# Layer norm by sums per token: shifted values, scalars as 128x4, and a spread by products with diagonals

## The chip, the cores and the metric

One core of a Trainium2 chip runs the whole program once. The metric is the time of an execution on the device in microseconds (us). Five engines work side by side, each through its own queue in order, and hand over to each other by semaphores: TensorE (PE, matrix products into PSUM banks), VectorE (DVE), ScalarE (ACT), GpSimd (POOL) and SyncE (SP), which only issues DMAs here.

## The reference

512 tokens of width 1024 pass through two layers (a pooling mixer and a sliding-window attention, each with a convolved, gated feed-forward of width 2816), a final norm, and a third layer: a conformer convolution and a squared-relu MLP of width 4096. The change is in the conformer convolution:

```
def layer_norm(x, g, b):
    mu = jnp.mean(x32, axis=-1, keepdims=True)
    xc = x32 - mu
    y = xc * lax.rsqrt(jnp.mean(xc * xc, axis=-1, keepdims=True) + RMS_EPS)
    return (y * g + b)
def conformer_conv(x, w_in, b_in, conv_w, conv_b, ln_g, ln_b, w_out, b_out):
    a, g = jnp.split(x @ w_in + b_in, 2, axis=-1)
    h = a * jax.nn.sigmoid(g)
    h = depthwise causal convolution of h over 31 tokens, + conv_b
    h = jax.nn.silu(layer_norm(h, ln_g, ln_b))
    return h @ w_out + b_out
```

## The kernel before

Activations lie with the 1024 features on partitions, as 8 chunks of 128 features x 512 tokens. Each f32 operand of a large product is split in a high part (`whi`, `xh`, rounded to fp32r by ACT, L799) and a low part (`wlo`, `xl`, the difference, by DVE, L1137), and a product is three (L475 to L477). A unit of weights is 128x1024; a chain is the 24 products of a unit, into one of the banks `acc[0..3]`. Weight units go through four slots: SP loads, ACT makes `whi`, DVE makes `wlo`.

The stage "ain" loops over the chunks c = 0 to 7 on every engine. PE (L755): the two chains of chunk c (values and gate), then `convolve(c - 1)`, then one product of ones with `hv` of chunk c - 2 into `norm[0]` (L751), which adds up the mean over all features, the same in every partition. DVE (L1509): evicts the two chains (L1527, `tmp`), makes the gated value `hc` (L1533), its low part `hcl` (L1545), and its share of the 31 taps. ACT (L1079): splits, the gate's sigmoid (L1091), `hch`, the high part of `hc` (L1100), the products of POOL's taps (`tapped`, L1074), and, for the convolution on PE, for each tap two 128x128 diagonals (L1059, L1061). POOL adds up `tapped` (L462). The 31 taps are divided by hand: `PE_TAPS`, `POOL_TAPS`, `LATE_TAPS` (done by DVE on the convolution's bank) and the rest, `own_taps`, on DVE in `bank[5]` (L1485 the first, L1488 the others). `collect` (L1500) adds the three partial sums to `hv` of the chunk.

After the loop the layer norm: the mean is subtracted from the eight chunks (L1555, DVE), ACT squares them (L1113), POOL and DVE add up some of the squares (L467, L1561), and PE sums them by products with ones (L770); root (L1115), reciprocal of 128x512 (L1564), a product for each chunk (L1567), Silu with slope and offset per feature (L1118), high and low parts `yhi` (L1121) and `ylo` (L1570, L1574). PE then runs the output projection "aout": its first two chains go feature block by feature block as `ylo` arrives (L775), the other six one after another. The reciprocal of `r1` (L1576), wanted by the residual in `finish` (L1168), stands behind the layer norm on DVE. Then follows the MLP.

A product of an f32 operand that isn't fp32r is shown as two instructions (two passes). At the very start of the kernel `token_sums` (L562) makes sums per token: the 128 features x 128 tokens of a block are the weights, and four columns (`pick`, one of them ones) are streamed.

Of the kernel before, what the change touches and what calls it, by code (L numbers as in the profile page):

```python
# [42 lines left out]
PE_TAPS = (9, 8, 7, 7, 7, 7, 12, 13)  # L43
POOL_TAPS = (11, 11, 11, 11, 11, 11, 10, 5)
# [105 lines left out]
def build(nc, xT, vec_in, cst_in, w_in, out):  # L150
# [3 lines left out]
    with ExitStack() as ctx:  # L154
# [37 lines left out]
        with ExitStack() as own:  # L192
# [4 lines left out]
            dgh = sb("dgh", [P, 2, max(PE_TAPS) * P], F32R, own)  # L197
            dgl = sb("dgl", [P, 2, max(PE_TAPS) * P], F32R, own)
# [10 lines left out]
        gfm = sb("gfm", [P, C])  # L209
        pbs = sb("pbs", [P, C])  # L210
# [5 lines left out]
        sq = sb("sq", [P, 2, T])  # L216
        u = sb("u", [P, 4, 2 + T])
# [7 lines left out]
        taps = bank[5]  # L225
# [66 lines left out]
        xc_ready = sem("xc_ready")  # L292
        xcsq_ready = sem("xcsq_ready")
        early_pair = sem("early_pair")
        late_sums = sem("late_sums")
# [40 lines left out]

        NORMS = ["pool", "ffn0", "qkv", "ffn1", "ain", "mlp"]
# [7 lines left out]
        RR = {"pool": 0, "ffn0": 1, "qkv": 2, "ffn1": 3, "ain": 4, "mlp": 7}  # L345
# [69 lines left out]
        def _(pool):  # L415
# [50 lines left out]
            pool.wait_ge(xcsq_ready, 4)  # L466
            nc.gpsimd.tensor_tensor(square_of(2), square_of(2), square_of(3), ALU.add).then_inc(early_pair, 1)  # L467
# [4 lines left out]
        def _(pe):  # L472
# [262 lines left out]
            def convolve(c):  # L735
# [5 lines left out]
                for k in range(PE_TAPS[c]):  # L741
                    w = slice(k * P, (k + 1) * P)
                    mm = three(bank[6 + b][:], dgh[:, b, w], dgl[:, b, w], hch[:, b, k:k + T],
                               hcl[:, b, k:k + T], k == 0, k == PE_TAPS[c] - 1)
                mm.then_inc(conv_done, 1)

            def feature_sum(c):
                if c == 0:
                    pe.wait_ge(rms_ready, RR["ain"] + 2)
                pe.wait_ge(hv_ready, c + 1)  # L750
                mm = nc.tensor.matmul(norm[0][:], ones[:], hv[:, c, :], start=(c == 0), stop=(c == C - 1))  # L751
                if c == C - 1:
                    mm.then_inc(mean_done, 1)
# [12 lines left out]
            feature_sum(C - 1)  # L766
# [361 lines left out]
        def _(dve):  # L1128
# [380 lines left out]
            for c in range(C):  # L1509
# [39 lines left out]
                if c:  # L1549
                    collect(c - 1)  # L1550
# [109 lines left out]
```

## Time and profile before

| | |
|---|---|
| time, median of 3 runs | 1498.51 us (1497.73 to 1498.73) |
| the profiled execution | 1498.34 us, of which span 1496.2 |
| busy PE / DVE / ACT / POOL | 98% / 63% / 44% / 14% |
| granted TensorE clock, mean | 0.994 |
| stage "ain" to the end of its last convolution | about 940 to 1078.5 us |
| from there to the first product of "aout" | to 1098.68 us |

A timeline row is: start us, length us, engine, line, operation, output<-inputs, shape, count, and in brackets how long the engine had sat idle before it and what released it. "x4" are four instructions merged. The granted clock is a share of 2.4 GHz.

### The profile page before, as it was taken

To read this page: it belongs to the slowest core of one execution; us is meant where nothing else is said; L and a number is where in the kernel's file an instruction comes from. 1 tells how busy PE (TensorE), PEld (TensorE's weight loads), DVE (VectorE), ACT (ScalarE), POOL (GpSimd) and SP (SyncE) were. 2 spreads that over 40 slices of the span, in tenths; PEclk is the share of its full clock that TensorE was granted. 3 is DMA by queue.
4 is the path that set the end of the run, shared out by engine and by line. 5 is a ranking of instruction groups with operands and counts; after the bars stand their busy time and mean duration, and the time that the engine had idled before them with its cause. 6 is when DMAs were issued, how large, how long until landed. Compare 5 with 4: busy or idle time off the path is not lost.

```text
span 1496.2 us, 20225 instructions
## 1 busy us (share of the span) xinstructions
PE 1463.8 (98%) x6878; PEld 1204.8 (81%) x6878; DVE 941.7 (63%) x1350; ACT 655.3 (44%) x1064; POOL 215.7 (14%) x155
## 2 busy tenths in 40 slices
PE   7999999999999999999999999999779999999999
PEld 7888888888877898888888887777558888888887
DVE  6877774573555667767735735898888763544532
ACT  5444441341546664444413415888754322222210
POOL 1200000000302241000000006498612000000000
PEclk9999999999999999999999999999989999999999
DMA  5222223232322012332332323111112322232321
GB/s 185 71 98 99 98 98 113 76 107 74 123 92 65 29 58 85 99 101 95 99 113 80 104 72 109 57 57 57 39 45 100 113 98 99 91 106 84 105 99 49
DMA packets 38956, 132.45 MB, mean 89 GB/s; under 512 B 4208, under 2 KB 4464, under 8 KB 38896
## 3 DMA queue, kind: packets, MB, share of 16 engines
q1 hardware_dynamic: 37888, 128.99, 26.2%
q10 hardware_dynamic: 1008, 2.69, 0.5%
q8 instruction: 35, 0.57, 0.2%
q14 instruction: 25, 0.20, 0.0%
HBM read 129.56 MB, written 2.10 MB: 88 GB/s over the span
## 4 chain that ended last, share of the span: by engine, by line
PE 85%; POOL 7%; ACT 4%; DVE 2%; issue 1%; ACTq 0%; POOLq 0%; DVEq 0%
PE bank L475 27%; PE bank L476 26%; PE bank L477 26%; POOL prod L462 5%; POOL ssum L434 2%; PE bank L557 1%; PE bank L618 1%; PE bank L646 1%; PE bank L631 1%; ACT dgl L1061 1%; ACT dgh L1059 1%; PE bank L580 1%; DVE bank L1488 1%; ACT whi L799 0%; ACT tapped L1074 0%
## 5 line engine op out<-in xcount | busy, mean ns | idle before, releaser
L475 PE MATMUL bank<-xh,whi 128*128 128x512 f32 x1184 | 465.9, 394 | 1.4 <-DVE res L1423 0.7
L477 PE MATMUL bank<-xh,wlo 128*128 128x512 f32 x1184 | 460.8, 389 | 0.0
L476 PE MATMUL bank<-xl,whi 128*128 128x512 f32 x1184 | 460.7, 389 | 0.0
L799 ACT ACTIVATE whi<-raw 128x1024 fp32r<-128x1024 f32 x244 | 255.7, 1050 | 232.6 <-PE bank L477 232.5
L1137 DVE TENSOR_TENSOR wlo<-raw,whi 128x1024 fp32r<-128x1024 f32 x244 | 305.4, 1252 | 57.0 <-ACT whi L799 49.4
L475 PEld LDWEIGHTS bank<-xh,whi 128*128 128x128 f32 x1184 | 222.3, 188 | 50.8 <-issue 3.1
L476 PEld LDWEIGHTS bank<-xl,whi 128*128 128x128 f32 x1184 | 222.3, 188 | 48.0 <-issue 2.4
L477 PEld LDWEIGHTS bank<-xh,wlo 128*128 128x128 f32 x1184 | 222.3, 188 | 46.4
L475 PE MATMUL bank<-ahi,whi 128*128 128x512 f32 x608 | 236.5, 389 | 0.0
L476 PE MATMUL bank<-alo,whi 128*128 128x512 f32 x608 | 236.5, 389 | 0.0
L477 PE MATMUL bank<-ahi,wlo 128*128 128x512 f32 x608 | 236.5, 389 | 0.0
L1158 DVE TENSOR_TENSOR res<-bank,res 128x512 f32 (+1 forms) x80 | 55.3, 691 | 201.5 <-PE bank L477 201.5
L434 POOL TENSOR_TENSOR ssum<-ssum,sq 128x512 f32<-128x512 f32 x40 | 62.4, 1561 | 759.4 <-ACT sq L818 418.8
L1208 DVE SCALAR_TENSOR_TENSOR tmp<-u,vec,tmp 128x512 f32<-128x512 f32 x176 | 124.2, 748 | 29.0 <-ACT tmp L856 28.9
L477 PEld LDWEIGHTS bank<-ahi,wlo 128*128 128x128 f32 x608 | 114.1, 188 | 23.8
L475 PEld LDWEIGHTS bank<-ahi,whi 128*128 128x128 f32 x608 | 114.1, 188 | 23.7
L476 PEld LDWEIGHTS bank<-alo,whi 128*128 128x128 f32 x608 | 114.1, 188 | 23.6
L856 ACT ACTIVATE tmp<-u,vec 128x512 f32<-128x512 f32 x88 | 71.7, 815 | 126.8 <-DVE u L1203 126.7
L1203 DVE TENSOR_TENSOR u<-bank,rinv 128x512 f32<-128x512 f32 x88 | 59.7, 686 | 68.4 <-PE bank L477 68.4
L462 POOL TENSOR_TENSOR prod<-prod,tapped 128x512 f32<-128x512 f32 x65 | 99.2, 1526 | 18.6 <-ACT tapped L1074 9.7
L878 ACT ACTIVATE ahi<-tmp 128x512 f32 (+1 forms) x32 | 20.2, 632 | 121.9 <-DVE tmp L1233 121.9
L860 ACT ACTIVATE gate<-tmp 128x512 f32<-128x512 f32 x44 | 27.9, 634 | 96.3 <-DVE tmp L1208 96.3
(175 smaller groups left out, 1439.2 us busy)
## 6 DMA issues: line engine op xcount, KB each, us to landing
raw<-w_ffn_up SPq DMA_DIRECT2D x88, 512.0 KB, 3.3
raw<-w_ffn_down SPq DMA_DIRECT2D x32, 512.0 KB, 3.3
raw<-w_mlp_up SPq DMA_DIRECT2D x32, 512.0 KB, 3.3
raw<-w_mlp_down SPq DMA_DIRECT2D x32, 512.0 KB, 3.3
raw<-w_ain SPq DMA_DIRECT2D x16, 512.0 KB, 3.3
raw<-w_ffn_down SPq DMA_DIRECT2D x16, 384.0 KB, 3.0
raw<-w_qkv SPq DMA_DIRECT2D x12, 512.0 KB, 3.2
raw<-w_wo SPq DMA_DIRECT2D x8, 512.0 KB, 3.3
```

Source lines behind the costliest of these rows:

```text
L434: nc.gpsimd.tensor_tensor(ssum[:, which, :], ssum[:, which, :], sq[:, buf, :], ALU.add)\
L462: nc.gpsimd.tensor_tensor(prod[:, c % 2, :], a, tapped[:, (made + k) % PARTS, :], ALU.add)\
L475: nc.tensor.matmul(out_, hi, mh, start=first, stop=False)
L476: nc.tensor.matmul(out_, hi, ml, start=False, stop=False)
L477: return nc.tensor.matmul(out_, lo, mh, start=False, stop=last)
L799: nc.scalar.activation(whi[:, s, 0:tiles * P], raw[:, s, 0:tiles * P], ACT.Copy)\
L856: nc.scalar.activation(tmp[:, k, :], u[:, k, 2:2 + T], ACT.Identity, scale=col(vec, par + 2), bias=col(vec, par + 3))\
L860: nc.scalar.activation(gate[:, b, :], tmp[:, 2 * b + 1, :], ACT.Silu)\
L1137: V.tensor_tensor(wlo[:, s, 0:tiles * P], raw[:, s, 0:tiles * P], whi[:, s, 0:tiles * P].bitcast(F32), ALU.subtract).then_inc(lo_done, 1)
L1158: V.tensor_tensor(row(res, c), acc[k][:], row(res, c), ALU.add).then_inc(acc_free, 1)
L1203: V.tensor_tensor(u[:, k, 2:2 + T], acc[k][:], rinv[:], ALU.mult).then_inc(acc_free, 1)
L1208: V.scalar_tensor_tensor(tmp[:, k, :], u[:, k, shift:shift + T], col(vec, par + 4 * j + shift), tmp[:, k, :], op0=ALU.mult, op1=ALU.add).t ...
```

## The change

- Chunk 0's mean (one product of ones with `hv` of chunk 0, in `norm[1]`, PE's loop step c = 2) is a common shift. DVE puts minus this mean in `rms`; the first own tap of chunks 2 to 7 becomes `hc * w + rms`, so that their `hv` come out shifted. Chunks 0 and 1 are shifted afterwards by DVE, in step c = 7.
- Sums of values and of squares are taken per token, like `token_sums`: sixteen groups of four products with eight streamed columns of `one_of`, into `norm[0][:, 0:8]`. Groups 0 to 3 stand in PE's steps c = 4 to 7 in the place of the mean products, groups 4 to 7 ahead of `convolve(7)`, groups 8 to 15 behind it. ACT makes the squares of chunks 2, 3, 0 and 1 in its step c = 7, the others after the loop; they lie in `sq` and `ssum`.
- Mean, variance, root, slope and offset are 128x4. Slope and offset are spread over partitions: DVE and ACT make diagonals of them, and PE multiplies ones with these into banks 5 and 6. A chunk is then a product and a sum on DVE (L1567 alone before).
- The own taps add up in `acc[0]` or `acc[2]`, with a wait of PE on `tap_steps` ahead of the chains; chunk 7 has 15 taps on PE (13 before), 4 on POOL (5), 12 own (13); two of its diagonals lie in storage of their own.
- "aout" runs three chains block by block, not two, after units 1 to 3 are split (1 and 2 before).
- The reciprocal of `r1` moves to DVE's step c = 0, after its own taps. The pair sums of squares on POOL and DVE, and the reciprocal of 128x512, go.

The core of the diff:

```diff
-PE_TAPS = (9, 8, 7, 7, 7, 7, 12, 13)
-POOL_TAPS = (11, 11, 11, 11, 11, 11, 10, 5)
+PE_TAPS = (9, 8, 7, 7, 7, 7, 12, 15)
+SPARE_TAPS = 2
+SHIFTED = 2
+POOL_TAPS = (11, 11, 11, 11, 11, 11, 10, 4)
...
+        SQUARES = (2, 3, 0, 1, 4, 5, 6, 7)
+        FIRST, SECOND = range(NBLK), range(NBLK, 2 * NBLK)
+        STATISTICS = [(2, FIRST), (3, FIRST), (4, FIRST), (5, FIRST), (2, SECOND), (3, SECOND), (0, FIRST),
+                      (0, SECOND), (1, FIRST), (1, SECOND), (4, SECOND), (5, SECOND), (6, FIRST), (6, SECOND),
+                      (7, FIRST), (7, SECOND)]
...
+                for b in range(NBLK):
+                    mm = nc.tensor.matmul(norm[0][:, 0:2 * NBLK], x[:, b * P:(b + 1) * P], pick_token_block(which[b]),
+                                          start=(n == 0 and b == 0), stop=(n == 2 * C - 1 and b == NBLK - 1))
+                mm.then_inc(sums_done, 1)
...
+                if c >= 2:
+                    pe.wait_ge(tap_steps, own_steps(c - 1))
                 for k in (2 * (c % 2), 2 * (c % 2) + 1) if c else ():
                     chain(p, c // 2, k, xh, xl)
                 if c >= 1:
                     convolve(c - 1)
-                if c >= 2:
-                    feature_sum(c - 2)
+                if c == 2:
+                    shift_sum()
+                if c >= 4:
+                    token_statistics(c - 4)
+            for n in range(4, 8):
+                token_statistics(n)
             convolve(C - 1)
-            feature_sum(C - 2)
-            feature_sum(C - 1)
...
+            for n in range(8, 2 * C):
+                token_statistics(n)
+
+            for at, ready, e in ((bank[5], slope_ready, 0), (bank[6], offset_ready, 1)):
+                for b in range(NBLK):
+                    pe.wait_ge(ready, b + 1)
+                    mm = nc.tensor.matmul(at[:, b * P:(b + 1) * P], ones[:], spread[:, e, b, :], start=True, stop=True)
+                mm.then_inc(spread_done, 1)
...
-                for k in range(2):
+                for k in range(3):
...
                 if c == C - 1:
                     products(c - 1, range(PARTS, POOL_TAPS[c - 1]))
+                    for e in SQUARES[0:3]:
+                        square(e)
                 products(c, range(min(PARTS, POOL_TAPS[c])))
...
+                if n == 0 and c < SHIFTED:
+                    V.tensor_scalar(part, x, w, None, ALU.mult).then_inc(tap_steps, 1)
                     return
...
+                V.scalar_tensor_tensor(hv[:, c, :] if n == len(own_taps(c)) - 1 else part, x, w,
+                                       part if n else rms[:], op0=ALU.mult, op1=ALU.add).then_inc(tap_steps, 1)
...
                 if c:
                     collect(c - 1)
+                if c == 0:
+                    V.reciprocal(r1[:], r1[:]).then_inc(rinv_ready, 1)
             collect(C - 1)
...
+            for b in range(NBLK):
+                V.tensor_scalar(spread[:, 0, b, :], ident, ln_slope[:, b:b + 1], None, ALU.mult).then_inc(slope_ready, 1)
+            split_lo(p.unit, 0, 2 * C - 1 + AHEAD)
             for c in range(C):
+                dve.wait_ge(spread_done, 1)
+                V.tensor_tensor(hv[:, c, :], hv[:, c, :], bank[5][:], ALU.mult).then_inc(ln_mul, 1)
+                dve.wait_ge(ln_mul, c + 1)
+                dve.wait_ge(spread_done, 2)
+                V.tensor_tensor(hv[:, c, :], hv[:, c, :], bank[6][:], ALU.add).then_inc(ln_scaled, 1)
```

## Rows read from the trace of the kernel before

**Rows 1.** page, part 1: busy us (share of the span) and instructions
```profile
PE 1463.8 (98%) x6878; PEld 1204.8 (81%) x6878; DVE 941.7 (63%) x1350; ACT 655.3 (44%) x1064; POOL 215.7 (14%) x155
```

**Rows 2.** windows: us; busy us (count) of PE, PEld, DVE, ACT, POOL; clock; DMA; GB/s
```profile
1010.00:1030.00 20.00, 19.92 (x86) 15.75 (x85) 19.35 (x25) 17.33 (x35) 18.57 (x12) 1.00 0.24 80
1067.50:1071.00 3.50, 3.41 (x8) 2.70 (x9) 3.43 (x6) 3.50 (x6) 3.21 (x3) 0.54 0.00 0
```

**Rows 3.** timeline of PE around the last convolution: start us, us, instruction, count, idle before
```profile
1063.74 1.02 PE L751 MATMUL bank<-hv,ones 128*128 128x512 f32 x2
...
1067.59 0.66 PE L475 MATMUL bank<-hch,dgh 128*128 128x512 f32 x1 [2.83 <-DVE hcl L1545]
...
1071.34 0.40 PE L475 MATMUL bank<-hch,dgh 128*128 128x512 f32 x1
...
1078.13 0.40 PE L477 MATMUL bank<-hch,dgl 128*128 128x512 f32 x1
...
1098.68 0.77 PE L475 MATMUL bank<-yhi,whi 128*128 128x512 f32 x1 [7.22 <-DVE ylo L1570]
```

**Rows 4.** timeline of POOL: the add before which it waited, first adds of two chunks
```profile
960.94 8.25 POOL L462 TENSOR_TENSOR prod<-prod,tapped 128x512 f32<-128x512 f32 x5 [2.41 <-ACT tapped L1074]
...
1020.02 1.30 POOL L462 TENSOR_TENSOR prod<-tapped 128x512 f32<-128x512 f32 x1
...
1037.03 1.30 POOL L462 TENSOR_TENSOR prod<-tapped 128x512 f32<-128x512 f32 x1
```

**Rows 5.** timelines of DVE and ACT: chunk 1's eviction and gate, and `r1`
```profile
956.00 1.28 DVE L1527 TENSOR_TENSOR tmp<-bank,rinv 128x512 f32<-128x512 f32 x2
...
958.59 0.71 ACT L1091 ACTIVATE gate<-tmp,vec 128x512 f32<-128x512 f32 x1
...
960.15 1.32 ACT L1074 ACTIVATE tapped<-hc,vec 128x512 f32<-128x512 f32 x2
...
1108.05 3.35 DVE L1576 RECIPROCAL r<-r 128x512 f32<-128x512 f32 x1
```

**Rows 6.** by line: duration ns min/median/max, first and last start, forms
```profile
L1533 DVE SCALAR_TENSOR_TENSOR hc<-tmp,vec,gate x8: 747/1268/1792, 947.8 to 1065.3; 128x512 f32<-128x512 f32 x8
...
L1485 DVE TENSOR_SCALAR bank<-hc,vec x8: 753/754/755, 948.6 to 1066.1; 128x512 f32<-128x512 f32 x8
```

**Rows 7.** timelines of DVE and POOL within one chunk
```profile
1025.91 1.35 DVE L1137 TENSOR_TENSOR wlo<-raw,whi 128x1024 fp32r<-128x1024 f32 x1 [0.40 <-ACT whi L799]
...
1027.18 1.78 DVE L1533 SCALAR_TENSOR_TENSOR hc<-tmp,vec,gate 128x512 f32<-128x512 f32 x1
...
1028.56 1.57 POOL L462 TENSOR_TENSOR prod<-prod,tapped 128x512 f32<-128x512 f32 x1
```

**Rows 8.** timeline of ACT: first diagonal, gate and products of chunk 7, four squares
```profile
1056.99 0.39 ACT L1059 ACTIVATE dgh<-cst,cwh 128x128 fp32r<-128x128 f32 x1
...
1064.60 0.71 ACT L1091 ACTIVATE gate<-tmp,vec 128x512 f32<-128x512 f32 x1
...
1066.68 5.70 ACT L1074 ACTIVATE tapped<-hc,vec 128x512 f32<-128x512 f32 x9
...
1085.15 2.42 ACT L1113 ACTIVATE tmp<-hv 128x512 f32<-128x512 f32 x4
```

**Rows 9.** timelines of PE, ACT and DVE at the start: sums by token, small steps
```profile
17.45 0.95 PE L566 MATMUL bank<-pick,sq 128*128 128x4 f32 x8
...
19.15 3.70 PE L557 MATMUL bank<-wg,res 128*128 128x256 f32 x16
...
24.57 0.26 ACT L943 ACTIVATE rms<-bank,eps 128x4 f32<-128x4 f32 x1 [5.58 <-PE bank L566]
...
24.86 0.18 DVE L1342 RECIPROCAL rinv<-rms 128x4 f32<-128x4 f32 x1 [4.10 <-ACT rms L943]
```

**Rows 10.** timeline of DVE in the layer norm: a split and a product
```profile
1090.20 1.22 DVE L1137 TENSOR_TENSOR wlo<-raw,whi 128x1024 fp32r<-128x1024 f32 x1
...
1098.46 0.68 DVE L1567 TENSOR_TENSOR hv<-hv,rinv 128x512 f32<-128x512 f32 x1
```

More of the change, by code:

```diff
@@ L209, in build @@
         gfm = sb("gfm", [P, C])
+        with ExitStack() as own:
+            one_of = sb("one_of", [P, 4 * NBLK], F32, own)
         pbs = sb("pbs", [P, C])
@@ L216, in build @@
         sq = sb("sq", [P, 2, T])
+        with ExitStack() as own:
+            dgh7 = sb("dgh7", [P, SPARE_TAPS * P], F32R, own)
+            dgl7 = sb("dgl7", [P, SPARE_TAPS * P], F32R, own)
         u = sb("u", [P, 4, 2 + T])
@@ L782, in _ @@
                         mm.then_inc(chain_done, 1)
-            for k in range(2, p.units):
+            for k in range(3, p.units):
                 chain(p, k // SLOTS, k % SLOTS, yhi, ylo)
@@ L1088, in _ @@
                     act.wait_ge(taps_split, 2)
-                    diagonals(0)
+                    diagonals(0, range(PE_TAPS[0]))
                 act.wait_ge(acc_free, p.chain + 2 * c + 2)
@@ L1110, in _ @@
             nc.scalar.activation(eps[:, 4:5], eps[:, 0:1], ACT.Sqrt)
-            for c in range(C):
-                act.wait_ge(xc_ready, c + 1)
-                nc.scalar.activation(square_of(c), hv[:, c, :], ACT.Square).then_inc(xcsq_ready, 1)
-            act.wait_ge(sqsum_done, 2)
-            nc.scalar.activation(rms[:], norm[1][:], ACT.Sqrt, scale=1.0 / D, bias=eps[:, 0:1]).then_inc(rms_ready, 1)
+            for e in SQUARES[4:]:
+                square(e)
+            act.wait_ge(ln_steps, 3)
+            nc.scalar.activation(ln_rms, ln_var, ACT.Sqrt, bias=eps[:, 0:1]).then_inc(ln_root, 1)
+            act.wait_ge(ln_steps, 5)
+            for b in range(NBLK):
+                nc.scalar.activation(spread[:, 1, b, :], ident, ACT.Copy, scale=ln_offset[:, b:b + 1])\
+                    .then_inc(offset_ready, 1)
+            nc.scalar.activation(eps[:, 4:5], eps[:, 0:1], ACT.Silu)
             for c in range(C):
@@ L1502, in collect @@
                 dve.wait_ge(tapped_steps, sum(POOL_TAPS[:c + 1]) - c - 1)
-                dve.wait_ge(tap_steps, sum(len(own_taps(j)) for j in range(c + 1)))
+                dve.wait_ge(tap_steps, own_steps(c + 1))
                 V.tensor_tensor(hv[:, c, :], prod[:, c % 2, :], hv[:, c, :], ALU.add).then_inc(late_steps, 1)
@@ L1529, in _ @@
                     split_lo(p.unit, 0, 2 * c + AHEAD)
+                if c == SHIFTED:
+                    dve.wait_ge(mean_done, 1)
+                    V.tensor_scalar(rms[:], norm[1][:], -1.0 / P, None, ALU.mult).then_inc(shift_ready, 1)
+                    dve.wait_ge(shift_ready, 3)
+                if c == C - 1:
+                    for e in range(SHIFTED):
+                        V.scalar_tensor_tensor(hv[:, e, :], norm[1][:], -1.0 / P, hv[:, e, :],
+                                               op0=ALU.mult, op1=ALU.add).then_inc(xc_ready, 1)
                 dve.wait_ge(sig_ready, c + 1)
@@ L1562, in _ @@
-            split_lo(p.unit, 0, 2 * C - 1 + AHEAD)
-            dve.wait_ge(rms_ready, RR["mlp"])
-            V.reciprocal(rinv[:], rms[:]).then_inc(rinv_ready, 1)
-            dve.wait_ge(rinv_ready, 8)
-            for c in range(C):
-                V.tensor_tensor(hv[:, c, :], hv[:, c, :], rinv[:], ALU.mult).then_inc(ln_scaled, 1)
+            dve.wait_ge(sums_done, 2 * C)
+            V.tensor_scalar(ln_mean, norm[0][:, 0:NBLK], 1.0 / D, None, ALU.mult).then_inc(ln_steps, 1)
+            dve.wait_ge(ln_steps, 1)
```

141 lines of the change are left out of this document (88 added, 53 removed).

## The prediction, made before the changed kernel was run

> **What bounds the kernel now.** Read the page first: TensorE (PE) is busy 1463.8 of 1496.2 us [rows 1], so an edit pays only where it shortens a place in which PE does not do the big products, and costs where it makes such a place longer. The slices of the page put the one such place at about 1064 to 1100 us, the end of the convolution stage and the layer norm. The windows before it, 1010 to 1030, have PE busy 19.92 of 20 and VectorE (DVE) 19.35 [rows 2]. PE's timeline then gives the place itself [rows 3]: the last convolution but one ends with the mean product of chunk 5 at 1063.74; PE waits 2.83 us for `hcl` of chunk 7; chunk 7's 13 taps (39 products) run from 1067.59 to the last at 1078.13 (over at 1078.5); the first product of `aout` starts at 1098.68. From there no row of PE shows a wait until the end. So the time is set by when `aout` can start, and by what its first chains then wait for. From the end of the chunk 7 convolution to that start are 20.2 us: this is what the change wants.
>
> Who sets the time of 1063.74? The chain of waits runs in that stage along GpSimd (POOL), whose adds follow each other: chunk 4's first add starts at 1020.02, chunk 5's at 1037.03, 17.0 us apart [rows 4], back to 960.94, where it last waited, 2.41 us, for ScalarE's (ACT) `tapped`. From POOL it goes to ACT: the diagonals of the next chunk stand behind a `tapped` that waits for POOL, and the gate stands behind the diagonals. Chunk 7's gate starts at 1064.60, directly after 26 diagonals that started at 1056.99 [rows 8].
>
> **Part A, the reciprocal of `r1`.** It takes 3.35 us [rows 5] at 1108, where PE computes, so taking it away there gives PE nothing. It moves to the end of chunk 0 on DVE. Queued behind it are the two evictions of chunk 1, which started at 956.00 and took 1.28; they now end at 960.7. ACT's gate of chunk 1 (958.59) waits for them: 960.7. Behind the gate are a split (959.20) and the `tapped` at 960.15 for which POOL waited [rows 5]. All move by 2.1 us, and POOL, which has no gap afterwards, passes this on. A = +2.1; the lower bound is 0, if PE and not POOL sets the pace.
>
> **Part B, the first own tap.** For chunks 2 to 7 it was a product of one SBUF tensor with a scalar and becomes one that also reads `rms` from SBUF. This is not the same 0.75 us. The old form (L1485) took 753 to 755 ns in all eight cases, mostly while POOL was adding; L1533, which reads two SBUF tensors, took 747 to 1792 [rows 6]. At 1027.18 it took 1.78, ending 1028.96, and POOL's next add took 1.57 instead of the 1.30 of an undisturbed one [rows 4, 7]. Whoever comes second waits until the other is done. The new tap comes straight behind L1533, when POOL has just started its add: by the same pattern DVE loses 1.03 and POOL 0.27. That is the smaller part. DVE has only 0.4 us idle in a chunk [rows 7], so its two later splits, `hcl` and collect come later against POOL's adds and hit them at other points. Walking one chunk with these durations, the second split meets a running add (1.0 us more for DVE) and POOL ends 0.5 to 0.7 late; walking a second, POOL loses 1.4, since DVE is by then late with the gate. Four such chunks (2 to 5) and a small hit in chunk 6 lie before chunk 7's gate. Lower bound 5 x 0.27 = 1.35, upper five times 1.4 = 7; I take 4, in the middle, because the second step of the walk already needs guesses on phase. If a two-input form that writes PSUM does not collide at all (all of the old ones that do write SBUF), B is 0; a gain isn't possible, nothing is taken away there.
>
> The Trainium skill (SBUF — State Buffer, "Who interferes with whom") says that a DVE instruction with two SBUF inputs contends with a GpSimd instruction that reads SBUF, and that the loser blocks fully. It makes no exception for a PSUM output, so by it B is not 0. The rows agree for SBUF outputs.
>
> **Part C, more diagonals.** Chunk 7 has 15 taps on PE instead of 13: four more ACT copies. 26 copies took 7.61 us [rows 8], 0.293 each, so the gate comes 1.2 us later. DVE's own taps fall from 13 to 12 and POOL's from 5 to 4, but neither will be last (below). The two subtractions of chunk 0's mean (2 x 0.68) lie in the time in which DVE waits for that gate, and cost nothing; the waits on `tap_steps` ahead of the chains ask for own taps that DVE has done by then, since it ends a chunk's taps before that chunk's successor is evicted. The mean product of chunk 1 falls away (about 0.9 us of PE, by the 1.02 of one with its end [rows 3]), those of chunks 2 to 5 are replaced one for one. POOL's pace swallows the gain.
>
> **Part D, what now stands ahead of chunk 7's convolution.** This is the largest term. PE's order has token sums 4 to 7 before the convolution, and three of these need ACT's squares of chunks 2, 3 and 0. ACT does these after `hch` of chunk 7 and after four `tapped` of chunk 6. In ACT's timeline the gate starts at 1064.60 and the `tapped` at 1066.68, 2.08 later; nine take 5.70, so four end 2.5 after that; a square takes 0.60 to 0.65 (four in 2.42) [rows 8]. The first square is ready 5.2 us after the start of the gate: 1064.60 + A 2.1 + B 4.0 + C 1.2 + 5.2 = 1077.1. Then four groups of sums. A group has four products in two passes, eight loads of 128x128 with few columns to stream; exactly this form is at the start of the kernel, with 4 columns in place of 8: two groups from 17.45 to 19.15, 0.85 us each [rows 9]. Four cost 3.4 at full clock. But PE has then idled some 6 us. After its idle of 2.83 us the granted clock was 0.54 between 1067.5 and 1071 [rows 2], that is 1.2 GHz nearly throughout, and the step of the products fell to its lasting value by 1071.34 [rows 3]. So I take 3.4 us at half speed (1.7 of work) and 1.7 at full, 5.1 together; ends 3.4 and 6.8. Convolution: 45 products x 0.234 (29 steps from 1071.34 to 1078.13 [rows 3]) = 10.5. It ends at 1077.1 + 5.1 + 10.5 = 1092.7, where it ended at 1078.5 before. Once it has, DVE and POOL have long finished.
>
> **Part E, the tail.** Eight groups of sums follow, 6.8 us, PE behind itself; the last square needs 2.4 us from the end of the convolution and is covered. Then, with 0.15 for the last product's end: three DVE steps on 128x4, a root, a reciprocal and an offset, at 0.18 and 0.26 a piece plus 0.04 between [rows 9] = 1.4; four diagonals of the slope on DVE, about 0.2 each (my estimate, from the 0.18 of 128x4) = 0.75; the split of `aout`'s third unit stands in DVE's queue behind them, 1.22 [rows 10]: 3.35. PE spreads slope and offset meanwhile. For chunks 0, 1 and 2 product and sum on DVE, 1.4 each, then the first `ylo`, 0.7 [rows 10]: 8.3 after the sums. ACT's Silu and copy of chunk 0 end at 6.2 and are covered. Together 15.3 us from the end of the convolution to `aout`, in place of 20.2: here the change gains 4.9. `aout` starts at 1108.0, 9.3 later than 1098.68.
>
> **Part F, three chains together.** Nine products a step take 2.05 us and DVE's three operations a step 2.1, with a lead, so PE doesn't wait. When the three end, PE needs the fourth unit's low part: DVE splits it behind the first eviction, which can start 1.2 us before PE ends. An eviction of 0.7 to 0.75, 1.22 and 0.1 of hand-overs, less 1.2, is 0.85 us of idle that the old order with two chains didn't have. I see no later wait: a step of `finish` is shorter than a chain of 5.5 us.
>
> Sum: 9.3 + 0.85 = +10.2 us on the profiled execution, 1496.2 us of span, 1498.34 with what lies around it: 1508.5. The median shown, 1498.51, is 0.01% above it, which changes nothing. A measurement of this kernel can tell about 0.2% (3 us).
>
> **Rivals.** (1) PE sets the pace of the stage and not POOL: A and B vanish. For it: PE is busy 19.92 of 20 [rows 2]. Against it: the period is that of POOL's adds. Then 10.2 - 6.1 = +4.1, 1502.4.
> (2) The other side: the sums cost next to nothing because only 8 columns stream and the loads slip under other work. At 0.2 us a group the twelve groups outside the loop cost 2.4 in place of 11.9: +0.7, 1499.0, no change. It decides from 0.39 us a group downwards (7.2 us saved). With (1) it would even be faster, 1493. Against it: the same form at 0.85 [rows 9].
> (3) DVE becomes the pacer of the loop, with B = 7 and the four early groups all at half clock: +14.9, 1513.2.
> (4) The change doesn't do what it says: the tail stays at 20 us because the small steps cost 1 us each and not 0.2. Then another +5 on the forecast, 1513.
>
> **How the numbers follow.** Forecast (A to F, B between 2 and 6) 0.57; rival 1 0.17, of this 0.05 at its low end, within 0.2%; rival 2 0.12, of this 0.07 together with 1 and faster; rival 3 0.09; rival 4 0.05. The range goes from the low end of rival 1 (early sums at full clock, 1500.7) to rival 3: 1500.5 to 1513.5. Faster 0.07, same 0.10, slower 0.83.
>
> **What would show it.** A: DVE evictions of chunk 1 at 959.4, POOL's wait ending near 963. B: the first own tap above 1 us in several of chunks 2 to 6, and POOL's distance between chunks above 17.2. C: 30 diagonals, 8.8 us. D: an idle of PE of some 6 us ahead of a sum of `sq`, then chunk 7's convolution ending 14 us later than before. E: about 15 us from there to `aout`. F: a wait of about 0.85 us on a split ahead of the fourth chain. Wrong would be: a chunk distance that stays at 17.0, sums at 0.4 us a group, or an `aout` that starts before 1098.7.

## The result, and the profile after

The changed kernel takes 1518.03 us (median of 4 runs, 1516.65 to 1519.07), against 1498.12 for the kernel before in the same comparison: a ratio of 1.0132, with a 95% interval of 1.0120 to 1.0145. It is slower, as forecast, by 19.9 us and not by 10.2, and lies outside the range that ended at 1513.5. The profiled execution has a span of 1517.1 us, 20.9 more than before [rows 1]; its mean granted clock is 0.988, where it was 0.994.

Read the same places as before. PE's timeline around the last convolution comes first; it answers to [rows 3]. Columns are those of the timeline: start, length, engine, line, operation, operands, shape, count, and the idle time before.

```profile
1068.23 0.95 PE L814 MATMUL bank<-one_of,hv 128*128 128x8 f32 x8
1075.49 3.58 PE L814 MATMUL bank<-one_of,sq 128*128 128x8 f32 x16 [6.31 <-ACT sq L1144]
1078.92 1.85 PE L814 MATMUL bank<-one_of,hv 128*128 128x8 f32 x8
1080.63 1.85 PE L814 MATMUL bank<-one_of,ssum 128*128 128x8 f32 x8
1082.34 0.77 PE L524 MATMUL bank<-hch,dgh 128*128 128x512 f32 x1
...
1095.31 0.39 PE L526 MATMUL bank<-hch,dgl 128*128 128x512 f32 x1
1095.54 0.95 PE L814 MATMUL bank<-one_of,hv 128*128 128x8 f32 x8
1096.35 1.04 PE L814 MATMUL bank<-one_of,ssum 128*128 128x8 f32 x8
1097.25 2.52 PE L814 MATMUL bank<-one_of,sq 128*128 128x8 f32 x16
1099.62 1.85 PE L814 MATMUL bank<-one_of,hv 128*128 128x8 f32 x8
...
1104.74 1.85 PE L814 MATMUL bank<-one_of,ssum 128*128 128x8 f32 x8
1108.17 3.78 PE L840 MATMUL bank<-tmp,ones 128*128 128x128 f32 x16 [1.58 <-DVE tmp L1666]
1116.14 0.77 PE L524 MATMUL bank<-yhi,whi 128*128 128x512 f32 x1 [4.19 <-DVE ylo L1676]
```

The wait of 6.31 us for `sq` is there. Then a group of eight loads takes 1.71 us (1078.92 to 1080.63), the last convolution needs 13.2 us, from 1082.34 to 1095.54, and of the eight groups behind it the first two need 0.81 and 0.90 us, the next two 2.37 together, and the last four 1.71 each. `aout` starts at 1116.14, 17.5 us later than in [rows 3]. The windows over the same stretch say why. Their columns are the window, its length, busy us (count) of PE, PEld, DVE, ACT and POOL, the granted clock, the DMA share and GB/s; [rows 2] are the windows of before.

```profile
1071.00:1075.40 4.40, 0.00 (x0) 0.00 (x0) 4.31 (x7) 3.59 (x7) 2.10 (x2) 0.51 0.00 0
1075.40:1082.30 6.90, 6.81 (x32) 6.82 (x33) 6.62 (x10) 6.88 (x11) 6.33 (x6) 0.50 0.01 2
1082.30:1086.00 3.70, 3.70 (x10) 2.93 (x11) 2.25 (x4) 2.31 (x5) 0.41 (x1) 0.50 0.00 0
1086.00:1088.20 2.20, 2.20 (x7) 1.72 (x6) 0.00 (x0) 0.00 (x0) 0.00 (x0) 0.51 0.00 0
1088.20:1095.50 7.30, 7.30 (x33) 5.93 (x32) 0.00 (x0) 0.00 (x0) 0.00 (x0) 1.00 0.00 0
1095.50:1098.40 2.90, 2.90 (x28) 2.86 (x27) 1.82 (x2) 0.63 (x1) 0.00 (x0) 1.00 0.00 0
1098.40:1106.50 8.10, 8.10 (x39) 8.09 (x39) 0.00 (x0) 0.00 (x0) 0.00 (x0) 0.50 0.20 65
```

The second row and the last are the point: PE is busy 6.81 of 6.90 and 8.10 of 8.10 us, and the clock is at its lower level, 1.2 GHz, throughout. In the second it was down from the idle time ahead of it, and it came up only 5.9 us into the convolution; in the last it fell during the sums, and PE had no idle time from 1075.49 on. The Trainium skill (TensorE: Matmul & The Clock Gate, Part 1, "The HAM clock gate") has the gate follow how busy PE has been; by that reading the last stretch would have stayed at full clock. Here the trace differs, and decides.

The loop of the stage answers to [rows 4] to [rows 7] in the timelines of DVE and POOL.

```profile
956.00 3.35 DVE L1651 RECIPROCAL r<-r 128x512 f32<-128x512 f32 x1
959.26 1.23 DVE L1618 TENSOR_TENSOR tmp<-bank,rinv 128x512 f32<-128x512 f32 x2
...
962.89 8.23 POOL L513 TENSOR_TENSOR prod<-prod,tapped 128x512 f32<-128x512 f32 x5 [4.37 <-ACT tapped L1155]
...
1015.37 8.12 POOL L513 TENSOR_TENSOR prod<-prod,tapped 128x512 f32<-128x512 f32 x5 [1.76 <-ACT tapped L1155]
1023.45 1.86 POOL L513 TENSOR_TENSOR prod<-tapped 128x512 f32<-128x512 f32 x1
...
1041.27 1.84 POOL L513 TENSOR_TENSOR prod<-tapped 128x512 f32<-128x512 f32 x1
```

POOL starts chunk 1's adds 1.95 us late, and first adds of neighbouring chunks are 17.8 us apart (1023.45 to 1041.27), where [rows 4] had 17.0. What lengthened stands in the durations by line (ns, least, median, most): the first own tap, the only one that reads `rms`, takes 1.74 us in the middle case, the others 0.75.

```profile
L1577 DVE SCALAR_TENSOR_TENSOR bank<-hc,vec,bank x46: 743/753/756, 949.9 to 1080.8; 128x512 f32<-128x512 f32 x46
L1577 DVE SCALAR_TENSOR_TENSOR bank<-hc,vec,rms x6: 759/1735/1832, 980.0 to 1071.8; 128x512 f32<-128x512 f32 x6
```

Four of the six take 1.67 to 1.83 us, while POOL adds. The other two, at 1052.00 and 1071.81, take 0.76: POOL was waiting when they began. Which engine paces the loop is seen from one period of POOL's adds, first before the change, then after it (columns of the windows as above):

```profile
1020.02:1037.03 17.01, 16.93 (x73) 13.25 (x72) 16.43 (x22) 14.34 (x29) 15.72 (x11) 1.00 0.19 62
1023.45:1041.27 17.82, 17.27 (x78) 13.73 (x78) 17.64 (x23) 14.35 (x29) 14.91 (x11) 1.00 0.17 54
```

DVE's work grew by 1.2 us a chunk. It had 0.58 us idle in a period and has 0.18 now, so the period grows by 0.8. ACT and POOL have some 3 us idle each.

Behind the layer norm PE waits twice for a weight split, where one such wait was forecast:

```profile
1136.34 0.50 PE L524 MATMUL bank<-yhi,whi 128*128 128x512 f32 x1 [0.75 <-DVE wlo L1228]
...
1164.55 0.50 PE L524 MATMUL bank<-xh,whi 128*128 128x512 f32 x1 [0.71 <-DVE wlo L1228]
```

### The profile page after: what moved, and what is told of

Read it like the earlier page. It is cut to its first block, busy times and chain, and to the rows that moved or that the text cites. A ratio compares the mean times of both kernels' runs of the same rounds, so it can differ in the third digit from the quotient of the medians.

```text
span 1517.1 us, 20505 instructions
## 1 busy us (share of the span) xinstructions
PE 1481.5 (98%) x7006; PEld 1227.5 (81%) x7006; DVE 943.7 (62%) x1359; ACT 657.0 (43%) x1072; POOL 211.1 (14%) x153
## 4 chain that ended last, share of the span: by engine, by line
PE 84%; DVE 6%; ACT 4%; POOL 3%; issue 2%; ACTq 0%; DVEq 0%; POOLq 0%
PE bank L524 26%; PE bank L525 26%; PE bank L526 26%; POOL ssum L485 2%; DVE wlo L1228 2%; POOL prod L513 1%; DVE bank L1577 1%; PE bank L814 1%; PE bank L606 1%; PE bank L667 1%; PE bank L695 1%; PE bank L680 1%; ACT dgl L1131 1%; ACT dgh L1130 1%; DVE res L1259 1%
## 5 line engine op out<-in xcount | busy, mean ns | idle before, releaser
L1228 DVE TENSOR_TENSOR wlo<-raw,whi 128x1024 fp32r<-128x1024 f32 x244 | 310.6, 1273 | 52.2 <-ACT whi L870 44.6
L513 POOL TENSOR_TENSOR prod<-prod,tapped 128x512 f32<-128x512 f32 x64 | 93.7, 1464 | 26.0 <-ACT tapped L1155 17.7
L949 ACT ACTIVATE ahi<-tmp 128x512 f32 (+1 forms) x32 | 20.2, 632 | 121.9 <-DVE tmp L1324 121.9
```

The lines of the kernel that those rows point to most:

```text
L513: nc.gpsimd.tensor_tensor(prod[:, c % 2, :], a, tapped[:, (made + k) % PARTS, :], ALU.add)\
L1228: V.tensor_tensor(wlo[:, s, 0:tiles * P], raw[:, s, 0:tiles * P], whi[:, s, 0:tiles * P].bitcast(F32), ALU.subtract).then_inc(lo_done, 1)
```

## The experiments

The disputed term is the cost of the few-column sums, so the first run takes only their shape away. Its theory is the clock: what a sum costs is not its own loads, it is the level that the clock keeps during it and after it. The rival is that PE's idle times and the loads by themselves make up the 10 us.

Executions come to this stage at slightly different times. The first `hc` starts at 947.81 in the changed kernel and in the kernel before, but at 947.02, 947.21, 947.46, 947.27, 947.62 and 947.11 in the six traces below, in their order. Where a place of one trace is compared with a place of another, 0.2 to 0.8 us of the difference can be this.

**Wide sums.** Each group is one product with ones over 512 columns, shown as two passes, of about the same length (0.86 us a group).

```diff
-                for b in range(NBLK):
-                    mm = nc.tensor.matmul(norm[0][:, 0:2 * NBLK], x[:, b * P:(b + 1) * P], pick_token_block(which[b]), ...)
-                mm.then_inc(sums_done, 1)
...
+                second = which is SECOND
+                nc.tensor.matmul(norm[int(second)][:], ones[:], x, ...).then_inc(sums_done, 1)
```

> The changed kernel, but each of the sixteen groups of sums is one product of ones (weights) with all 512 columns, as the old mean products: the same 0.86 us of TensorE at full clock, but columns streamed instead of weights loaded. The statistics that come out are then those of tokens 0 to 3 for all blocks, so the normalisation is computed wrongly; every instruction around it is kept. Theory 1 (products of eight columns do not keep TensorE's clock up, though the engine is busy): the convolution of chunk 7 takes 10.5 to 11.5 us in place of 13.2, the eight sums behind it 6.9 in place of 10.95, and the first aout product comes 7 to 9 us earlier: about 1509 to 1511. Rival (the clock follows the long wait of 6.3 us for the squares, whatever the sums look like): the times stay within 2 us of 1518.

Measured: 1508.84, ratio 1.0075 (1.0058 to 1.0092). PE's timeline, and then the windows of the four groups and of the eight (columns as above):

```profile
1074.74 3.78 PE L816 MATMUL bank<-sq,ones 128*128 128x512 f32 x4 [6.21 <-ACT sq L1145]
...
1091.39 1.02 PE L816 MATMUL bank<-hv,ones 128*128 128x512 f32 x2
...
1106.38 0.47 PE L524 MATMUL bank<-yhi,whi 128*128 128x512 f32 x1 [4.33 <-DVE ylo L1677]
```

```profile
1074.70:1080.60 5.90, 5.86 (x9) 2.53 (x9) 5.65 (x8) 5.90 (x9) 5.43 (x5) 0.55 0.00 0
1091.40:1098.30 6.90, 6.90 (x17) 2.83 (x15) 1.82 (x2) 0.63 (x1) 0.00 (x0) 1.00 0.22 76
```

The wait of 6.21 is unchanged, but the convolution takes 10.9 us and not 13.2, and eight groups of the same work in time (6.90 us) keep the clock at 1.00. `aout` starts 9.8 us earlier than in the changed kernel (9.0 without the 0.8 by which this execution was ahead). It is shown that 9.2 us of the time hang on the shape of the sums. The first window sets a limit to this: behind the long wait the wide sums ran at the lower clock too, for the first 5.3 us, and took 5.76 us where the small ones took 6.85. So the low clock there comes with the wait. What the shape decides is that the clock was up again when the convolution began, and that it stayed up in the eight groups.

**All sums behind the last convolution.** This takes away the wait for the squares ahead of it.

```diff
-            for n in range(4, 8):
-                token_statistics(n)
             convolve(C - 1)
-            for n in range(8, 2 * C):
+            for n in range(4, 2 * C):
```

> The changed kernel, with groups 4 to 7 behind the convolution of chunk 7 instead of ahead of it. Both theories: the convolution starts at about 1073.2 when hcl is ready, not at 1082.3. Theory 1 (clock): twelve groups follow on each other, three or four at 0.85 us and the others at 1.7, so 15 to 18 us; sums done at 1101 to 1103 instead of 1106.5, time about 1513 to 1515. Rival (place alone is at fault, the sums would run at 0.85 us if they did not stand behind a long wait): sums done at about 1096, time about 1508.

Measured: 1512.99, 1.0105 (1.0086 to 1.0123). The convolution starts at 1072.68, 9.7 us earlier; the twelve groups behind it start at 1084.63 and the clock falls among them, at 1089.3, with PE busy without a gap since 1072.68 (the trace has 11.50 of 11.50 us at 0.50 from 1089.3 to 1100.8). The spread starts only at 1102.47, 5.7 us earlier. The time falls by 5.0 us, half of the 10 that the order alone should give; the clock keeps the rest.

**Each step alone undone.** Three runs put back the reciprocal (A), the plain first tap (B), and A, B and the 30 diagonals (C) together.

```diff
-                if c == 0:
-                    V.reciprocal(r1[:], r1[:]).then_inc(rinv_ready, 1)
...
+            V.reciprocal(r1[:], r1[:]).then_inc(rinv_ready, 1)
             dve.wait_ge(rinv_ready, 8)
```

> The changed kernel with the reciprocal of r1 back behind the layer norm on VectorE (step A undone). By A: GpSimd resumes at 960.9 instead of 962.9 and everything behind moves by 2.0 us, time about 1516. Rival (TensorE sets the pace of the stage, a late eviction is absorbed): no change, 1518.

Measured: 1513.27, 1.0110 (1.0093 to 1.0126). Chunk 7's gate starts at 1068.01, 2.27 earlier than the 1070.28 of the changed kernel; less the 0.35 by which this execution was ahead, A is 1.92. The time fell by 4.8, where 2 were expected. In the two profiled executions the rest goes with the clock: their spans differ by 6.1 us, and PE worked 22.3 us in windows at 0.50, where the changed kernel had 30.8, which is worth half of 8.5. In this trace the clock held through the first 5.3 us of the eight groups, in the changed kernel through 2.9. Whether the edit did this or the execution is open.

```diff
-                if n == 0 and c < SHIFTED:
+                if n == 0:
...
-                                       part if n else rms[:], op0=ALU.mult, op1=ALU.add)
+                                       part, op0=ALU.mult, op1=ALU.add)
```

> The changed kernel with the first own tap of every chunk as before (a product with a scalar, no rms read), and the shift of chunks 0 and 1 multiplied by zero, so no value is shifted; all instructions are kept in number (step B undone). By B: the chunk distance of GpSimd is 17.0 instead of 17.8 us, chunk 7's gate 2.5 us earlier, time about 1515.5. Rival (the distance grew for another reason, the wait on tap_steps or the banks of the own taps): 17.8 and 1518.

Measured: 1514.51, 1.0107 (1.0090 to 1.0124). POOL's timeline has the period of before again, 17.0 us, and no wait:

```profile
1004.42 1.30 POOL L513 TENSOR_TENSOR prod<-tapped 128x512 f32<-128x512 f32 x1
1005.86 15.62 POOL L513 TENSOR_TENSOR prod<-prod,tapped 128x512 f32<-128x512 f32 x9
1021.44 1.30 POOL L513 TENSOR_TENSOR prod<-tapped 128x512 f32<-128x512 f32 x1
```

The gate comes at 1067.11, 3.17 earlier; less the 0.54 by which this execution was ahead, B is worth 2.6 us. The second input from SBUF is shown to be what lengthens the loop. The Trainium skill (SBUF — State Buffer, "Who interferes with whom") has a DVE instruction with two SBUF inputs contend with a GpSimd instruction that reads SBUF, and makes no exception for a result in PSUM. Here the trace agrees: the result goes to PSUM, and it takes 1.74 us against 0.75.

```diff
-PE_TAPS = (9, 8, 7, 7, 7, 7, 12, 15)
+PE_TAPS = (9, 8, 7, 7, 7, 7, 12, 13)
...
-POOL_TAPS = (11, 11, 11, 11, 11, 11, 10, 4)
+POOL_TAPS = (11, 11, 11, 11, 11, 11, 10, 5)
...
```

(The edits of the last two runs are in it as well.)

> The changed kernel with steps A, B and C undone: reciprocal of r1 behind the layer norm, first own tap without rms (no value shifted), chunk 7 with 13 taps on TensorE, 5 on GpSimd and 13 on VectorE. By my sum the three add up: 1.9 + 2.6 + 1.2 = 5.7 us ahead of chunk 7's gate and 1.4 us of convolution, so about 1511 and the gate at 1064.6 as before the change. What is left (about 12 us over the kernel before) is then the place of the sums, the clock and the end of the stage. Rival (the three share one slack, undoing one is enough): 1513 to 1514, the gate at 1066 or later.

Measured: 1510.73, 1.0085 (1.0068 to 1.0101). The gate is at 1064.42, where it was before the change [rows 8], so A, B and C are the whole of what happens in the loop. The rest of the loss, 12.7 us by the ratio, comes from D, E and F.

**The same groups between the taps.** Groups 4 to 11 stand between taps 6 to 14 of the last convolution, three products of 512 columns after each; nothing else changes, and no column is added.

```diff
+                    if c == C - 1 and 6 <= k < 14:
+                        token_statistics(k - 2)
                     mm = three(bank[6 + b][:], diagonal(cwh, c, k), ...)
...
-            for n in range(4, 8):
-                token_statistics(n)
             convolve(C - 1)
-            for n in range(8, 2 * C):
+            for n in range(12, 2 * C):
                 token_statistics(n)
```

> The changed kernel with groups 4 to 11 of the sums between the taps 6 to 14 of the convolution of chunk 7, one ahead of each tap's three products of 512 columns; four groups stay behind it. Clock theory: between full products the sums run at 0.85 us and the clock stays up after the first 3.5 us; convolution and eight groups together 19 us from 1073 on, then four groups in 3.4 to 5: sums done at 1096 instead of 1106.5, time about 1507 to 1509. Rival (a burst of eight loads lowers the clock wherever it stands, or loads and products of two kinds hold each other up): 24 us or more for the mixed stretch, time at 1514 or above.

Measured: 1508.00, 1.0069 (1.0052 to 1.0085), 10.0 us less than the changed kernel, and 5.0 less than with all groups behind. Its timeline of PE for one period, and the window over eight:

```profile
1085.12 0.95 PE L816 MATMUL bank<-one_of,hv 128*128 128x8 f32 x8
1085.93 0.47 PE L524 MATMUL bank<-hch,dgh 128*128 128x512 f32 x1
1086.24 0.40 PE L525 MATMUL bank<-hcl,dgh 128*128 128x512 f32 x1
1086.48 0.39 PE L526 MATMUL bank<-hch,dgl 128*128 128x512 f32 x1
1086.70 0.95 PE L816 MATMUL bank<-one_of,ssum 128*128 128x8 f32 x8
```

```profile
1080.00:1092.00 12.00, 12.00 (x83) 10.92 (x82) 3.98 (x6) 3.94 (x6) 2.07 (x2) 1.00 0.00 0
```

The group takes 0.8 us until the next product, the full-clock price, and 12 us of such a mixture keep 1.00. The four groups behind the convolution held the full clock here too (3.70 of 3.70 us at 1.00, from 1092.1). Of the places for these sums that were run this is the best; it also lets the convolution start without the wait for the squares, so the gain over the changed kernel isn't the clock's alone.

**Rebuilt from the steps that held.** No common shift, `r1` behind the layer norm, 13 taps on PE for chunk 7, the sums of values in PE's loop, the squares where ACT waits for POOL, most groups ahead of or within the last convolution, and the splits of `aout`'s third and fourth unit ahead of the sums and of the first eviction.

```diff
-                if c >= 4:
-                    token_statistics(c - 4)
-            for n in range(4, 8):
+                if c >= 2:
+                    token_statistics(c - 2 if c < C - 1 else 7)
+            for n in range(8, 10):
...
+                    if k == PARTS - 1 and 3 <= c < C - 1:
+                        square(c - 3)
```

> A version built from the findings: scalars as 128x4 and the spread are kept, the shift is left out altogether (sums of unshifted values and squares; the same normalisation), reciprocal of r1 behind the layer norm, 13/5/13 taps for chunk 7; sums of values one group for one old mean product; squares of chunks 0 to 3 by ScalarE where it waits for GpSimd, their groups in the two gaps of TensorE ahead of the convolutions of chunks 6 and 7; groups of 4 and 5 within the last taps; four groups behind the convolution. The third unit is split ahead of the sums, the fourth ahead of the first eviction, and four products of the residual with r1 ahead of the loop of finish. If place and clock of the sums were the loss, the convolution ends at about 1079 to 1080, the sums at 1084 to 1087, the first aout product comes at 1091 to 1095 against 1098.7 in the kernel before: time 1491 to 1496. Rival (the spread with its handshakes and the double operation for each chunk cost what the 128x512 steps did): aout at 1098 or later and 1498 or more.

Measured: 1496.00, 0.9985 (0.9975 to 0.9995). A little faster than the kernel before, by 0.15%. So sums per token need not cost anything where they are well placed; how much of the gain is theirs and how much that of the splits was not run apart. `aout` starts at 1094.23, 4.5 us earlier than in [rows 3], but the span is only 2.9 us shorter. Of the difference 1.2 us is the clock in the first chains: PE worked 5.4 us at 0.50 from the start of `aout`, and 3.1 before the change.

**Order of the layer norm on DVE.** The second product ahead of the first sum, the first `ylo` directly behind the third product.

```diff
-                if c >= 2:
-                    dve.wait_ge(ln_hi, c - 1)
-                    V.tensor_tensor(ylo[:, c - 2, :], hv[:, c - 2, :], ...)
...
+            for step in "ppssp", "ls", "pls", "pls", "pls", "pls", "pls", "ll":
+                for what in step:
```

(p, s and l are the next chunk's product, sum and `ylo`.)

> The version rebuilt from the steps that held, with one change of order on DVE in the layer norm: the first two products stand ahead of the first sum, so that DVE does not wait for the spread offset with nothing to do (0.83 us there), and the first `ylo` stands directly behind the third product, where ACT's `yhi` is ready (it ended at 1092.35 in y1_rebuilt, DVE took it up at 1093.40). If the start of the output projection waits for this one queue, its first product comes 0.7 to 1.2 us earlier after the spread and the whole kernel gains about 1 us: 1495. If ScalarE is late instead, or the granted clock decides the first 6 us of the projection anyway, nothing moves: 1496.

Measured: 1494.88, 0.9978 (0.9969 to 0.9987), some 1 us less, with intervals that overlap. PE's idle time ahead of `aout` fell from 4.19 to 3.18, and a wait of 1.09 us for the fourth unit's split appeared.

**Unread wide products, 25 of them.** Also between the last groups.

```diff
                 token_statistics(n)
+                wide(2 if n < 2 * C - 1 else 7)
...
+            wide(12)
```

> As y2_reordered, and PE does work that nobody reads wherever it would stream few columns or wait: two products of 512 columns behind each of the last three-but-one groups of sums, seven behind the last, twelve behind the spread, into a bank that nobody uses then (25 products, 5.8 us at full clock, of which 1.4 stand on the path and the others lie in idle time of 1.6 and 3 to 4 us). Theory of the clock: the granted clock stays at or near 1.00 from 1078 to the end of the block-by-block chains, so the spread takes 1.8 in place of 3.5 us, the two groups of sums at 1.2 GHz take 0.85 again, and the first chains lose nothing (steps of 0.233 from the start, about 3 us gained over y1_rebuilt): 1490 to 1492. Rival: the clock falls there in any case (from the idle time before the 7th convolution or for another reason): then the fillers cost up to 1.4 to 4 us, 1497 to 1500.

Measured: 1498.28 (1494.65 to 1501.91), 0.9999 (0.9988 to 1.0009). A miss. In the profiled execution, one of the seven of eleven that took 1498.3 us or more, the clock fell at 1082.6 all the same, with PE busy before and in it, and it rose again at 1092.9. The other four took 1494.7 to 1496.4, and what the clock did in them isn't known.

```profile
1077.20:1082.60 5.40, 5.40 (x41) 5.02 (x41) 4.57 (x6) 1.26 (x2) 0.84 (x1) 1.00 0.00 0
1082.60:1092.90 10.30, 10.30 (x39) 9.24 (x39) 2.79 (x11) 3.06 (x7) 0.00 (x0) 0.50 0.32 103
```

So wide products between the groups do not in themselves hold the clock, and at the lower level the fillers on the path take twice as long (seven in 3.1 us, from 1087.70 to 1090.84). The chains of `aout` did run at full clock from their first product, and what this brought forward went into a wait of 3.36 us for the fourth unit's split, which stands on DVE behind the reciprocal and four scaled residuals.

**That split first.** This and what follows builds on the version with the new order, without the 25 wide products.

```diff
-                                split_lo(p.unit, i, k + AHEAD)
...
+            split_lo(ph["aout"].unit, 0, AHEAD)
             V.memset(ssum[:], 0.0).then_inc(ssum_ready, 1)
             V.reciprocal(r1[:], r1[:]).then_inc(rinv_ready, 1)
```

> y2_reordered with the split of the fourth unit of the output projection directly behind the last `ylo`, and not behind the reciprocal of `r1` (3.29 us) and four scaled residuals (2.74). PE waited 1.09 us for that split at 1114.05. If that wait costs what it shows, it goes, and the time is 1.1 us lower: 1493.8. Rival: the evictions that now come behind the reciprocal are late in its place, and PE waits for a bank further on: 1495.

Measured: 1493.32, 0.9977 (0.9967 to 0.9987). The ratio is that of the version with the new order (0.9978), so no gain is shown. The wait of 1.09 is gone, and one of 0.34 stands a chain later.

**And unread products only where PE waits.** Four behind the last group, eight behind the spread.

```diff
                 token_statistics(n)
+            wide(4)
...
+            wide(8)
```

> y4_split_first with unread products of 512 columns only where PE waits in any case: four behind the last group of sums (PE idled 1.58 us there) and eight behind the spread (3.18 us idle). In y3_filled the first `aout` products ran at full clock (steps of 0.23 where y2_reordered had 0.43 for 4.8 us) and the 3.36 us that this brought forward were lost again in the wait for the fourth unit's split, which is gone here. If the idle time is what keeps the clock down at the start of the projection: 2 to 3 us below y4_split_first, 1491. Rival: the clock there depends on the execution and not on 12 products: as y4_split_first, within 1 us.

Measured: 1493.33, 0.9978 (0.9967 to 0.9989): nothing gained. But the traces are not the same. First the timeline of PE with the split first, then with the fillers, each at the start of `aout` and at the next wait:

```profile
1091.20 0.76 PE L524 MATMUL bank<-yhi,whi 128*128 128x512 f32 x1 [3.18 <-DVE ylo L1690]
...
1116.25 0.50 PE L524 MATMUL bank<-yhi,whi 128*128 128x512 f32 x1 [0.34 <-DVE wlo L1235]
```

```profile
1090.65 0.47 PE L524 MATMUL bank<-yhi,whi 128*128 128x512 f32 x1 [1.33 <-DVE ylo L1696]
...
1115.68 0.50 PE L524 MATMUL bank<-yhi,whi 128*128 128x512 f32 x1 [2.99 <-DVE wlo L1241]
```

The clock was 0.50 in the first from 1083.3 to 1096.9 and in the second only until 1086.7. The first chains gained some 3 us, and a wait of 2.99 us one chain later took them. It is for the fifth unit: ACT makes its high part behind a wait for the first eviction (9.34 us idle), and DVE the low part behind that.

**The splits of the finish one unit earlier.**

```diff
-                        split_hi(p.unit, i, k + AHEAD)
+                        if SLOTS * i + k < C - 1:
+                            split_hi(p.unit, i, k + 1 + AHEAD)
                         act.wait_ge(acc_free, p.chain + SLOTS * i + k + 1)
...
-                        if not out_bias or c:
+                        if not out_bias:
                             split_lo(p.unit, i, k + AHEAD)
+                        elif c < C - 1:
+                            split_lo(p.unit, i, k + 1 + AHEAD)
```

> y5_split_and_fill with the weight splits in the stage that finishes the output projection one unit earlier on ACT and DVE: ACT makes the high part of the fifth unit when the first chain is over and not behind its wait for the first eviction (it idled 9.34 us there), and DVE its low part directly behind that eviction, ahead of `xl`. In y5_split_and_fill the first products ran at full clock and all three chains ended 3 us earlier than in y4_split_first, and PE then waited 2.99 us at 1115.68 for that low part. If that wait was all that ate what the clock gave back: 1490 to 1491. Rival: the DVE's queue in this stage is full (2.9 us a chunk against 5.46 of PE speaks against it) or the clock falls elsewhere: 1493, as y5_split_and_fill.

Measured: 1491.89 (1490.08 to 1492.48), 0.9951 (0.9937 to 0.9965). This beats both kernels: 6.4 us less than before in the same comparison, 26 less than the changed one. Its trace is that of the longest of the five executions, the one of the version before it that of the shortest. `aout` starts 3.4 us later in it (1094.01) and the span is only 0.4 us longer (1490.4 against 1490.0): the wait of 2.99 is what was gained. After the first product of `aout` PE has no wait there any more; the windows from there on (us, PE busy, clock, DMA share, GB/s) are full:

```profile
1110.00:1115.00 5.00, 5.00 (x24) 1.00 0.01 3
1115.00:1120.00 5.00, 4.97 (x22) 1.00 0.31 105
1120.00:1125.00 5.00, 5.00 (x23) 1.00 0.56 187
```

Whether the twelve unread products earn anything once the splits are early was not run by itself. Nor was the old layer norm with these early splits, so the 6.4 us belong to the whole of the edits and not to the sums per token alone.

## Why the prediction was right or wrong

- **What bounds the kernel, and the direction**: right. The loss lies where PE does not do the big products, or does them at the lower clock: 17.5 of 20.9 us ahead of `aout`, the rest behind its first product. Rival 1 is refuted, since undoing A and B each moved the gate, and rival 2 by 0.81 us a group at the least.
- **A**: right. 2.1 foreseen, POOL's start moved by 1.95, and undoing it moved the gate by 1.92 (2.27 as read, with 0.35 from an earlier start of the stage).
- **B**: mechanism right, also for PSUM output. 4 was too high: of the gate's 5.68 us, 2.55 remain after A and C, and undoing it gave 2.6, in the lower half of 1.35 to 7. The sign for it was right too (a distance above 17.2), but not where I put it: POOL's own adds don't add up to more (1.9, 5.95 and 8.1 are 16.0 a chunk, 16.9 with the plain tap), it waits 1.76 us a chunk for `tapped`. DVE paces the loop, as in rival 3, busy 17.64 of 17.82 us, and it costs 0.8 us a chunk and not 1.4. That DVE had 0.4 us idle in a chunk stood in the prediction; it had 0.58, and that is what the longer tap used up first.
- **C**: four diagonals more, 1.17 us against 1.2. The gate is 5.7 late in all and not 7.3.
- **D**: the wait was right: the first sum starts 5.21 us after the gate, as forecast 5.2. The step that failed is the one after it, "3.4 us at half speed (1.7 of work) and 1.7 at full". The clock didn't rise while few-column sums ran, so the four groups took 6.85 and not 5.1 (+1.75), and the convolution that I had begin at full clock spent its first 5.9 us at the lower level: 13.2 and not 10.5 (+2.7). The first run splits this: with wide sums the four groups took 5.76 and the convolution 10.9. So 1.1 and 2.3 hang on the shape; 0.65 is that the clock stays down longer after this wait than I took, whatever the sums (5.3 us and not 3.4).
- **E**: the same fault, larger. I took eight groups at 0.85, the number of [rows 9], where only two follow each other. They took 10.95 us (+4.15). The small steps cost what I said (0.16 to 0.18 each). The spread was "meanwhile": at the lower clock its 16 products take 3.78 us and DVE waits 0.45 and 1.09 for them; with the ends that is +1.15. The tail has 20.6 us in place of 15.3, no gain against the 20.2 of before. Rival 4 named that number for another reason (steps of 1 us), which the 0.16 to 0.18 refute; that it comes out near is luck.
- **F**: 0.75 against 0.85 for the wait that was named. A second of 0.71 was missed. The MLP starts with two chains together and needs the split of DVE's seventh step of `finish`: six steps of 4.7 us behind the first, 28.2, where PE has only the five chains that are left, 27.3. My sentence that a step is shorter than a chain compared one with one and not their sums. With the first chains held up by the lower clock 1.5 us more than before, and 0.5 not traced to a line, this is +2.6 on F.

The balance: 10.2, less 1.6 for A to C, plus 4.45 for D, 5.3 for E and 2.6 for F, is 20.9, the difference of the spans. Of the 12.3 us by which D to F were missed, the shape of the sums accounts for 9.2 by the first run. Most of the error was one number: 0.85 us a group came from a row where the form was over after two groups; that a long run of the form could bring the clock down, or keep it down, was no case of mine. The trace of before had a second stretch at the lower clock, behind the last convolution (window, length, busy us (count) of PE, clock, DMA share, GB/s):

```profile
1081.40:1088.20 6.80, 5.36 (x6) 0.50 0.24 77
```

There PE also had idle times of 1.39, 0.20 and 1.44 us between sums of 512 columns, so it would not have told what the small sums do, but it was a reason not to take the tail at full clock.

## What to carry to other kernels

Price a form by a row in which it runs for as long as you mean to run it, and look at the granted clock of that window; in the traces here a series of small products kept the full clock for its first 2.3 to 5.3 us (between two and six groups), and then it and what followed ran at the lower one. Single groups between large products kept it for 12 us. Where PE is brought forward, look at once at what the next queue was doing: here gains of 1 to 3 us came back as a wait for a split, until that too was moved.

## What the runs showed of the hardware

- The clock can fall while PE is busy without a gap: 8.10 of 8.10 us at 0.50 in 128x8 sums; 6.90 of 6.90 at 1.00 with 128x512 sums of the same length; 12.00 of 12.00 at 1.00 with the small ones between taps. When it falls differs: 2.3 us after the first of the eight groups in the trace with the plain tap, 5.3 us in that with `r1` put back.
- After a wait of 6.2 to 6.3 us the clock stayed at its lower level for 5.3 us of busy PE with 128x512 sums, and for 12.7 us with 128x8 sums and then taps.
- Two wide products behind each group did not hold it (10.30 us busy at 0.50); taps of the convolution between the groups did, in one kernel. Why the one and not the other is open. Where the lower stretch ends also differs between executions: it was 1086.7 with the twelve unread products and 1091.4 in the next kernel with the same twelve, so a single trace does not settle what they are worth.
- A 128x512 operation of DVE with two inputs from SBUF, writing PSUM, takes 1.74 us beside POOL's adds (0.75 for one input; 0.76 for two where POOL was waiting), and costs the loop 0.8 us a chunk.
